# ScalarE takes the root of the head norm before, not after, the next projection's evictions

## The reference

```python
def readout(o_f, o_b, g):
    Bn, T = g.shape[:2]
    o = rmsnorm(o_f + flip(o_b), gain).reshape(Bn, T, HG_WIDTH)
    return (o * jax.nn.silu(g.astype(jnp.float32))).astype(g.dtype)
```

## Time and profile before

| | us |
| --- | --- |
| median of the runs | 3191.41 |
| lowest, highest | 3189.16, 3192.23 |
| profiled execution, its own time | 3190.96 |
| its span | 3189.1 |
| TensorE busy (matmuls) | 3046.8 |
| VectorE busy | 1543.6 |
| ScalarE busy | 1000.1 |
| GpSimd busy | 450.3 |

### The profile page before, as it was taken

How to read it: one execution, slowest core, us unless ns; L and a number is a source line. 1 busy time by engine, 2 the same in 40 slices (tenths; PEclk the granted TensorE clock), 3 DMA queues, 4 the chain that set the end, 5 groups by cost and what they waited for, 6 DMA issues and landing times.

```text
span 3189.1 us, 36113 instructions
## 1 busy us (share of the span) xinstructions
PE 3046.8 (96%) x14927; PEld 2487.1 (78%) x14927; DVE 1543.6 (48%) x1907; ACT 1000.1 (31%) x1441; POOL 450.3 (14%) x352
## 2 busy tenths in 40 slices
PE   8899999989999999999989999999898999999997
PEld 6688888878788888888866668888776888888886
DVE  7566666553565553433566764456644122222224
ACT  5555555552311122212423332233322111111111
POOL 4333333321000001000300002133300000000001
PEclk9999999999999999999999999999999999999999
DMA  3111111122233431111210001101131111111111
GB/s 124 40 47 47 47 47 47 47 67 99 65 115 121 129 120 52 49 51 47 94 54 7 9 10 48 34 21 40 47 112 31 56 47 47 52 47 47 50 43 60
DMA packets 77235, 184.75 MB, mean 58 GB/s; under 512 B 7056, under 2 KB 29072, under 8 KB 77072
## 3 DMA queue, kind: packets, MB, share of 16 engines
q1 hardware_dynamic: 77072, 182.44, 18.2%
HBM read 163.87 MB, written 15.79 MB: 56 GB/s over the span
## 4 chain that ended last, share of the span: by engine, by line
PE 86%; DVE 8%; ACT 4%; issue 2%; POOL 0%; DMA 0%; POOLq 0%; DVEq 0%; SPq 0%; ACTq 0%
PE ps L512 39%; PE ps L1604 18%; PE ps L2950 8%; PE ps L2291 4%; DVE b L2899 2%; PE ps L2429 1%; PE ps L909 1%; PE ps L2255 1%; PE ps L2284 1%; PE ps L2283 1%; DVE b L501 1%; PE ps L916 1%; ACT b L493 1%; PE ps L86 1%; PE ps L891 1%
## 5 line engine op out<-in xcount | busy, mean ns | idle before, releaser
L512 PE MATMUL ps<-b 128*128 128x512 f32 x6024 | 1494.9, 399 | 35.6 <-DVE b L501 14.0
L512 PEld LDWEIGHTS ps<-b 128*128 128x128 f32 x6024 | 1109.9, 190 | 251.2 <-issue 19.9
L1604 PE MATMUL ps<-b 128*128 128x512 f32 x2592 | 599.1, 392 | 0.7 <-DVE b L1745 0.7
L1604 PEld LDWEIGHTS ps<-b 128*128 128x128 f32 x2592 | 485.0, 187 | 109.3 <-DVE b L1745 1.1
L501 DVE TENSOR_TENSOR b<-b 128x1024 fp32r<-128x1024 f32 (+1 forms) x206 | 255.3, 1241 | 288.3 <-ACT b L493 280.9
L493 ACT ACTIVATE b<-b 128x1024 fp32r<-128x1024 f32 (+1 forms) x206 | 214.9, 1045 | 515.9 <-PE ps L1604 427.4
L2950 PE MATMUL ps<-b 128*128 128x512 f32 (+1 forms) x1464 | 327.3, 379 | 6.8 <-ACT b L3010 5.9
L2950 PEld LDWEIGHTS ps<-b 128*128 128x128 f32 x1464 | 255.0, 192 | 56.5 <-issue 11.5
L1402 POOL TENSOR_TENSOR b<-b 128x1024 f32<-128x1024 f32 x18 | 43.2, 2399 | 916.8 <-ACT b L1433 916.4
L2291 PE MATMUL ps<-b 128*128 128x512 f32 x320 | 163.0, 592 | 0.0
L1761 DVE TENSOR_TENSOR b<-b,ps 128x1024 f32<-128x1024 f32 x64 | 78.1, 1220 | 152.4 <-PE ps L1604 152.3
(11 more groups left out here) (306 smaller groups left out, 3292.8 us busy)
## 6 DMA issues: line engine op xcount, KB each, us to landing
b<-in_down SPq DMA_DIRECT2D x52, 512.0 KB, 3.7
b<-in_mod SPq DMA_DIRECT2D x96, 256.0 KB, 2.7
b<-in_gu SPq DMA_DIRECT2D x44, 512.0 KB, 3.6
b<-scratch SPq DMA_DIRECT2D x38, 512.0 KB, 4.4
b<-in_dn_in SPq DMA_DIRECT2D x32, 512.0 KB, 5.1
b<-in_up SPq DMA_DIRECT2D x32, 512.0 KB, 3.8
b<-in_win SPq DMA_DIRECT2D x26, 512.0 KB, 3.7
scratch<-b SPq DMA_DIRECT2D x18, 512.0 KB, 2.9
```

The lines of the kernel that those rows point to most:

```text
L512: ins = e.matmul(ps[:, c], w, h[:, k, c], start=first and k == 0 and i == 0, stop=last and k == KT - 1 and i == 2)
L1604: ins = e.matmul(ps[:, c], w, u[:, at[k], c], start=k == 0 and p == 0, stop=k == n - 1 and p == 2)
```

## The change

In `act_gla` the fill of six steps that stood between the squares and the root moves behind the root.

```diff
             e.wait_ge(*V.at("oc", h))
             e.activation(B["sq"], B["qf"], ACT.Square).then_inc(*A.up("osq", h))
-            side.fill(self.gla_fill(h, 6))
             self.act_roots(e, A)
             e.wait_ge(*V.at("oms", h))
             e.activation(small[:, 8:16], small[:, 0:8], ACT.Sqrt).then_inc(*A.up("ort", h))
+            side.fill(self.gla_fill(h, 6))
             side.until((h, "g"))
```

## The result

The changed kernel takes 3180.78 us (median of 6 runs, 3179.5 to 3186.32), the kernel before 3192.53 us beside it (6 runs). The ratio is 0.9966 with a 95% interval of 0.9956 to 0.9976: 10.9 us faster, with 7.7 and 14.0 as bounds (the two medians by themselves are 11.8 us apart). The forecast was 3180.4. The profiled execution took 3180.62 us, its span is 3178.8 us; that is 10.3 us less than the profiled execution of the kernel before.

What follows compares the result with a forecast made beforehand. TensorE, busy 96% of the span, was taken as the bound, so only its standstills pay. 7.6 (standstills) + 3.0 (clock) + 0.5 (table load) = 11.1 us, giving 3180.4 us for the median, range 3176.5 to 3186.0.

Steps and rivals of the forecast that it cites:

- The standstill of 7.6 us: TensorE's L79 waits 2.54 us for VectorE's reciprocal in each of heads 0 to 2; all 7.6 us go.
- Evictions behind the root cost nothing: hq's two ScalarE evictions, now behind root and SiLU load, still start when their matmuls are done; cost zero.
- covers of 0.8 and 1.1 us: Head 0: evictions have 0.8 us to spare before starting late, then another 1.1 us before TensorE waits.
- The clock, 3.0 us: Low-clock stretches behind L79 in heads 0 and 1 are caused by the standstills and go: 3.0 us together.
- the cap in head 0: L2416's input, ready at 2064.80, lets only 0.72 us more count beside L79's 0.54: 1.3 us in head 0.
- The table load, 0.5 us: Three SiLU loads in the levels go, two hidden; head 2's TensorE wait for evictions goes, 0.5 us.
- Rival B: Only standstills and the table-load wait go, slow clock comes in other places: 8.1 us, 3183.3 us; chance 0.30.
- Rival C: Something in VectorE's chain from L79 to the key sum stays in place, losing 2.5 us: 3185.8 us; chance 0.09.
- Rival D: Mean square over 4.8 us later delays evictions, stopping TensorE at the first matmul behind L79: 3200.5 us; chance 0.02.
- Rival E: L79 waits for something other than the root, so nothing moves: 3191.4 us; chance 0.03.

Runs made afterwards that it cites:

- The late runs: Changed kernel with 4, 6 or 10 VectorE copies ahead of the mean square in heads 0 to 2, delaying the root: 3181.28, 3188.35, 3198.11 us.
- six copies: Changed kernel with six VectorE tile copies ahead of the mean square in heads 0 to 2, root about 4.2 us later: 3188.35 us, ratio 0.9990.
- the filled ones: Kernel before with 11 unused matmul products in each standstill of heads 0 to 2, run twice: 3192.21 us, then 3188.44 us.
- four copies: Changed kernel with four VectorE tile copies ahead of the mean square in heads 0 to 2, root 2.8 us later: 3181.28 us, ratio 0.9967.
- keys early: Changed kernel with VectorE's five key instructions for the next head moved right behind the reciprocal: 3182.03 us, ratio 0.9969.

## Why the prediction was right, point by point

*The standstill of 7.6 us goes entirely.* Shown: none of it is left, and with one head moved at a time, head 2, which had no low clock to give back, brought 2.72 us for its 2.54.

*Evictions behind the root cost nothing.* Shown: they still wait 0.82 us for TensorE in heads 0 and 2, 1.73 in head 1; I had worked out 0.8 for head 0. The late runs show the cover's size: with 2.8 us of lateness the evictions hold TensorE for 0.68, 0.30 and 0.67 us. The worked-out covers of 0.8 and 1.1 us would leave 0.9, of which the late L79 hides 0.3. With 4.3 us of lateness a head costs 2.1 to 2.2, and most of the gain is lost. The Trainium skill (ScalarE: Activation LUTs, "What ACT_TABLE_LOAD costs") has a drain of about 1.4 us on top of a load; with six copies the load started 0.02 us after the root's end and the eviction 1.29 us after the load's start, which leaves no room for one on either side.

*The clock, 3.0 us.* The working holds for gaps 0 and 1: 3.77 and 4.79 gained against 3.8 and 4.7, down to the cap in head 0, where I let the key sum stop the gain (TensorE now waits 0.39 us for it). That the standstills cause the low clock behind them is shown by the filled ones, which won 1.0 and 1.6 us in the gaps in both profiles; the medians say 0 in the first set of runs and 3.0 us in the second. What I missed is the other sign: low clock that comes anew elsewhere. In the levels behind head 2 it came for 1.6 us behind a wait of 2.30 us that both kernels have. That this wait draws it is not shown, since no run filled it: over all profiles the low clock followed it in 6 of 13 cases, always in the changed kernel as it is and with the load put back, but not with four copies in the same order. So of the 11.1 us forecast, 9.7 came in the stretch I had worked out. Of the 10.3 us between the two profiled executions the other 0.6 is what low clock behind head 3 took and gave; the ratio's 10.9 differs from 10.3 by less than single executions spread. Over everything behind head 0's output copy but the very end, the low clock lasts for about 24 us before (from 2056, 2159, 2312, 2350 and 2432) and about 20 in the changed kernel (from 2278, 2302, 2418 and 3159), 17 in its second profile; at half speed the first pair gives an estimate of 2 us of work won back, not 3.0. The total agrees better than the terms do, and that is partly luck: where the low clock falls behind head 2 and head 3 was not worked out.

*The table load, 0.5 us.* Shown, 0.48, by putting it back.

*Rival B* (only the standstills go) was half right in kind: both stretches behind the standstills went, and filling shows that they need not come, but low clock does turn up elsewhere, one new stretch for two in the gaps.

*Rival C* (something given back) did not come; the chain behind L79 moved up as a whole, and the key sum cost 0.4 us more.

*Rival D.* Its point and price were near: I put the turning point at 4.8 us of lateness; between the runs at 4.3 (3188.35) and 7.2 (3198.11) a straight line crosses the time of before on that chip (3191.2) at 5.1. For 7.3 us of lateness I had 3200.5; 7.2 us gave 3198.11. But its mechanism was wrong in the main: I had the banks, held by the late evictions, as what stops TensorE, and it is L79 waiting for the late root; the evictions add 0.7 us a head at most. A root that waits for a mean square 7.2 us later would be late in the old order too, and rival D sets the late new order against an old order that is not late. The agreement of the numbers is therefore no support for it as a price of the order. *Rival E* (no effect) is out.

## What to carry to other kernels

Where an in-order engine has a tiny instruction on another engine's path and a larger one that must wait for that other engine anyway, the tiny one goes first: the larger still starts when its input is there, and only the surplus of the wait decides. Price the standstill, and the clock behind it, as two terms, and check them with useless work in the gap: it tells them apart without touching the dependency. A gain of the second kind can come back as a loss elsewhere: here all that follows moved up, and low clock turned up behind a wait that had none before.

## What the runs showed of the hardware that was not expected

A standstill of 2.54 us on TensorE was followed by a stretch of TensorE at the 1.2 GHz level in 5 of 7 cases. In head 1 it was in the kernel before and was not with head 0 moved, with the same instructions around it. A standstill of 3.8 to 4.7 us was followed by it in 3 of 3, one of 0.9 to 1.8 us (six copies) in 0 of 3, and a gap filled with matmuls in 0 of 9. Longer is not always worse: the wait of 3.11 us behind head 3 stands in all fourteen profiles, and the L79 behind it ran slowly, 1.94 us in place of 1.06, in three of them (the kernel before, six copies, keys early). A float32 product of 128x128 by 128x128 is two matmul records of 0.11 us each. VectorE's copy of 128x1024 float32 took 0.69 us from SBUF to SBUF and 1.22 us out of PSUM.
